# A hybrid attention and PEER layer in float32: the expert stage's schedule by fixed rules, and GpSimd's low parts on VectorE

## The reference

```python
qh = (xt @ w_query).reshape(T, PEER_HEADS, PEER_KEY_DIM)
s1 = jnp.einsum('thd,nd->thn', qh[..., :half], sub_keys_1)
s2 = jnp.einsum('thd,nd->thn', qh[..., half:], sub_keys_2)
v1, i1 = lax.top_k(s1, PEER_TOPK)
v2, i2 = lax.top_k(s2, PEER_TOPK)
cand = (v1[..., :, None] + v2[..., None, :]).reshape(T, PEER_HEADS, PEER_TOPK * PEER_TOPK)
top_s, top_j = lax.top_k(cand, PEER_TOPK)
experts = jnp.take_along_axis(cand_idx, top_j, axis=-1)
gate = jax.nn.softmax(top_s)
a = jax.nn.gelu(jnp.einsum('cd,ced->ce', xc, expert_u[experts]))
y = jnp.einsum('ce,ced->cd', gate * a, expert_v[experts])
```

## Time and profile before

| | |
|---|---|
| median of three executions | 1001.05 us |
| the three | 1001.03, 1001.05, 1006.59 us |
| the profiled execution | 1006.59 us, span 1004.7 us |
| busy share of the span | PE 98%, weight loads 86%, DVE 74%, ACT 51%, POOL 31% |
| chain that ended last | 88% of the span is L473, the matmul helper |

### The profile page before, as it was taken

How to read it: one execution, slowest core, us unless ns; L and a number is a source line. 1 busy time by engine, 2 the same in 40 slices (tenths; PEclk the granted TensorE clock), 3 DMA queues, 4 the chain that set the end, 5 groups by cost and what they waited for, 6 DMA issues and landing times.

```text
span 1004.7 us, 17520 instructions
## 1 busy us (share of the span) xinstructions
PE 986.5 (98%) x6258; PEld 865.1 (86%) x6258; DVE 745.7 (74%) x1865; ACT 517.3 (51%) x1107; POOL 311.6 (31%) x370
## 2 busy tenths in 40 slices
PE   8999999999999999999999999999999999999996
PEld 3467865999999999999999999988888888888885
DVE  1167353789999788889999999766666766666668
ACT  1245342233445788888888888543334333343341
POOL 1000000000220699999999999000000000000000
PEclk9999899999999999999999999999999999999998
DMA  9833200683555455445454454665555555556551
GB/s 328 330 125 148 84 22 1 213 320 124 183 190 179 157 169 168 164 153 168 167 166 155 166 168 157 242 231 193 197 196 189 193 198 195 191 189 195 201 169 43
DMA packets 48758, 176.52 MB, mean 176 GB/s; under 512 B 5136, under 2 KB 6176, under 8 KB 47520
## 3 DMA queue, kind: packets, MB, share of 16 engines
q1 hardware_dynamic: 48272, 173.82, 50.6%
q0 software_dynamic: 400, 1.58, 0.4%
HBM read 174.33 MB, written 1.05 MB: 175 GB/s over the span
## 4 chain that ended last, share of the span: by engine, by line
PE 90%; DVE 7%; ACT 1%; issue 1%; DMA 1%; SPq 0%; DVEq 0%
PE ps L473 88%; DVE lo L1491 1%; PE ps L657 1%; DVE pair L1679 1%; DVE arena L1624 1%; DMA arena<-in_w_tok 1%; DVE hi L1491 1%; DVE arena L1629 0%; DVE arena L1632 0%; ACT hi L1050 0%; DVE slab L1689 0%; DVE xs L1768 0%; DVE xs L1762 0%; DVE arena L1756 0%; DVE xs L1753 0%
## 5 line engine op out<-in xcount | busy, mean ns | idle before, releaser
L473 PE MATMUL ps<-x1hl,hi 128*128 128x256 f32 x2248 | 374.1, 283 | 0.6 <-DVE hi L1491 0.6
L473 PEld LDWEIGHTS ps<-x1hl,hi 128*128 128x128 f32 x2248 | 330.4, 192 | 0.9 <-DVE hi L1491 0.8
L473 PE MATMUL ps<-hi,ahl 128*128 128x512 f32 x992 | 265.3, 389 | 0.0
L1198 ACT CAST hi<-slab 128x1024 fp32r<-128x1024 f32 x128 | 135.0, 1055 | 204.8 <-PE ps L473 204.6
L473 PE MATMUL ps<-x1hl,lo 128*128 128x256 f32 x824 | 233.2, 283 | 0.0
L473 PEld LDWEIGHTS ps<-hi,ahl 128*128 128x128 f32 x992 | 186.1, 188 | 38.7
L455 POOL TENSOR_SCALAR hot<-slab 128x128 fp32r<-128x128 f32 x224 | 197.7, 898 | 0.0
L473 PEld LDWEIGHTS ps<-x1hl,lo 128*128 128x128 f32 x824 | 158.2, 192 | 0.0
L1712 DVE TENSOR_TENSOR lo<-slab,hi 128x1024 fp32r<-128x1024 f32 x128 | 156.0, 1218 | 0.0
L473 PE MATMUL ps<-lo,ahl 128*128 128x512 f32 x496 | 152.8, 389 | 0.0
L1491 DVE TENSOR_TENSOR lo<-slab,hi 128x1024 fp32r<-128x1024 f32 x97 | 121.8, 1257 | 18.9 <-ACT hi L1050 18.4
(11 more groups left out here) (199 smaller groups left out, 910.2 us busy)
## 6 DMA issues: line engine op xcount, KB each, us to landing
slab<-in_uT SPq DMA_DIRECT2D x128, 512.0 KB, 3.3
slab<-in_pv SPq DMA_DIRECT2D x128, 512.0 KB, 3.3
arena<-in_wq SPq DMA_DIRECT2D x32, 512.0 KB, 4.8
arena<-in_w_tok SPq DMA_DIRECT2D x2, 2048.0 KB, 16.3
arena<-in_w_out SPq DMA_DIRECT2D x1, 4096.0 KB, 13.7
arena<-in_w_tok SPq DMA_DIRECT2D x4, 512.0 KB, 8.4
arena<-in_w_tok SPq DMA_DIRECT2D x1, 1792.0 KB, 19.1
slab<-in_xT SPq DMA_DIRECT2D x4, 256.0 KB, 7.4
```

The costliest lines, as they stand in the source:

```text
L473: return nc.tensor.matmul(o, lhsT, rhs, start=start, stop=stop, skip_group_check=True)
L1198: nc.scalar.copy(hi[:, v_hi_slot(c), :], raw[:, v_slot(c), :]).then_inc(v_hi, 1)
```

## The change

Three things change together. The table FILL_AT and the step counter go: each place in the routing code now has a fixed rule for whether a low part is made there (`fills`, or a condition on the half t). GpSimd makes no low parts any more; VectorE makes all. And the numbers of the schedule differ: N0 33 to 41, NROUTE 29 to 36, NTURN 30 to 37, and the groups stand at 41 + g*21//16, which like before ends at block 123. In the first half (t = 0) five low parts are made, in the eight sub-key calls of the second half two each, in its route() fifteen.

```diff
-N0 = 33
-NROUTE = 29
-NTURN = 30
-FILL_AT = (54, 55, 57, 66, 68, 68, 76, 79, 79, 86, 89, 89, 97, 99, 99, 106, 109, 109, 119, 120, 120, 123, 124,
...
+N0 = 41
+NROUTE = 36
+NTURN = 37
...
-POOL_LOW = range(5, 26, 3)
-GROUP_AT = [N0 + g * (123 - N0) // 63 for g in range(GN)]
+GROUP_AT = [N0 + g * 21 // 16 for g in range(GN)]
...
-            for c in POOL_LOW:
-                pool.wait_ge(u_hi, c + 1)
-                nc.gpsimd.tensor_tensor(u_rest_of(c), u_raw(c), hi[:, c % UH, :].bitcast(F32), ALU.subtract
-                                        ).then_inc(u_lo_pool, 1)
             pool.wait_ge(table_ready, 1)
...
             def expert_in(c):
-                if c in POOL_LOW:
-                    pe.wait_ge(u_lo_pool, pool_lows(c))
-                else:
-                    pe.wait_ge(u_lo, c + 1 - pool_lows(c))
+                pe.wait_ge(u_lo, c + 1)
...
-                    if c not in POOL_LOW:
-                        dve.wait_ge(u_hi, c + 1)
-                        v.tensor_tensor(u_rest_of(c), u_raw(c), hi[:, c % UH, :].bitcast(F32), ALU.subtract).then_inc(u_lo, 1)
+                    dve.wait_ge(u_hi, c + 1)
+                    v.tensor_tensor(u_rest_of(c), u_raw(c), hi[:, c % UH, :].bitcast(F32), ALU.subtract).then_inc(u_lo, 1)
                     filled[0] += 1
 
-            steps = [0]
-
-            def pace():
-                steps[0] += 1
-                while filled[0] < NROUTE and FILL_AT[filled[0]] == steps[0]:
-                    fill()
-
-            def top16(jobs):
+            def top16(jobs, fills):
                 for o in (0, 8):
                     for vals, _, s in jobs:
                         did(v.max(vals[:, o:o + 8], s))
-                    pace()
+                    if o and fills > 2:
+                        fill()
                     settle()
                     for vals, idx, s in jobs:
                         did(v.max_index(idx[:, o:o + 8], vals[:, o:o + 8], s))
-                    pace()
+                    if fills:
+                        fill()
                     if o == 0:
                         settle()
                         for vals, _, s in jobs:
                             did(v.match_replace(s, vals[:, 0:8], s, TAKEN))
-                        pace()
+                        if fills > 2:
+                            fill()
...
-                top16([(tv[:, hh, :], ti[:, hh, :], cand[:, hh, :]) for hh in range(PH)])
+                if t:
+                    fill()
+                settle()
+                top16([(tv[:, hh, :], ti[:, hh, :], cand[:, hh, :]) for hh in range(PH)], 4 * t)
...
-                    pace()
+                    if t or part and h0:
+                        fill()
...
                     did(v.tensor_reduce(tfp, eqh, AX_X, ALU.add))
-                    pace()
+                    fill()
...
-                subkey_tops(1, b)
+                subkey_tops(1, b, 2)
```

More of the change, by code:

```diff
@@ L37 @@
 PI_IN = 3.1415925
-N0 = 33
-NROUTE = 29
-NTURN = 30
-FILL_AT = (54, 55, 57, 66, 68, 68, 76, 79, 79, 86, 89, 89, 97, 99, 99, 106, 109, 109, 119, 120, 120, 123, 124,
-           124, 127, 128, 129, 130, 131,)
+N0 = 41
+NROUTE = 36
+NTURN = 37
 GN = S // 4
@@ L321, in peer_layer_kernel @@
         u_hi, u_lo, v_hi, v_lo = sem("u_hi"), sem("u_lo"), sem("v_hi"), sem("v_lo")
-        u_lo_pool = sem("u_lo_pool")
         pe_h, gelu_done, pre_gated, gated = sem("pe_h"), sem("gelu_done"), sem("pre_gated"), sem("gated")
@@ L355, in u_rest_of @@
             return lo[:, b, :] if b < 4 else hi[:, 3, :]
-        def pool_lows(c):
-            return sum(b <= c for b in POOL_LOW)
         def v_slot(c):
@@ L1513, in top16, with subkey_tops @@
                             did(v.match_replace(s, vals[:, 0:8], s, TAKEN))
-                        pace()
+                        if fills > 2:
+                            fill()
                     settle()
-            def subkey_tops(t, b):
+            def subkey_tops(t, b, fills):
                 dve.wait_ge(sk_saved, 2 * PH * t + b + 2)
-                top16([(V[:, t, i, :], IX[:, t, i, :], sc[t][:, i, :]) for i in (b, b + 1)])
+                top16([(V[:, t, i, :], IX[:, t, i, :], sc[t][:, i, :]) for i in (b, b + 1)], fills)
             dve.wait_ge(trig, 2)
@@ L1594, in _ @@
             for b in range(0, 10, 2):
-                subkey_tops(0, b)
+                subkey_tops(0, b, 0)
             def route(t):
@@ L1700, in block_gate @@
                 v.tensor_tensor(a, gel[:, c % 2, 0:n], a, ALU.mult).then_inc(gated, 1)
-            assert filled[0] == NROUTE and steps[0] >= FILL_AT[-1]
+            assert filled[0] == NROUTE
             while filled[0] < N0 - 1:
```

## The result

The changed kernel takes 1011.61 us (median of 4, 1011.3 to 1012.46) beside 1002.63 us (median of 4, 1001.03 to 1006.59) for the kernel before: a ratio of 1.0084, 95% interval 1.0058 to 1.0109. It is slower, by a little less than 1%. The profiled execution took 1011.38 us, its span 1009.5 us.

The account below looks back on a forecast made before the run. GpSimd, nearly level with TensorE in the gates' stage, would set the pace: start at 355.4 us plus 283.6 us of work puts the last gates at 639.2 instead of 632.22, +7.0 on 1001.05, so 1008.0 us, range 1003 to 1014.

Parts of the forecast that it names:

- VectorE keeps up in routing: Routing window: VectorE makes all 36 low parts, 84.8 us of work for 89.3 us of blocks, without TensorE waiting.
- the 0.73 us: TensorE's wait before 327.92 us for a late VectorE low part in the kernel before; forecast to go.
- The margin of 0.8 us at the second routing pass: Start of second routing pass, the tightest place: VectorE 2.2 us late, under the 3.0 us of room.
- Transposes at block 37: Route transposes move from block 30 to 37, starting at 349.96 us; routes ready some 7 us ahead.
- GpSimd's first one-hot 5.4 us after the transposes, and its end as start plus work: Gates' stage: GpSimd starts at 355.4 us, 21.1 later, and ends at 639.0 after 283.6 us of work.
- A wait at block 40 of about 1 us: ScalarE's pairs stand ahead of block 40's cast; low part ready at 360.3 us, block due at 359.3.
- GpSimd's 283.6 us, 4.43 a group: Gates' stage: 290.6 us of GpSimd work less eight subtractions at 0.87 us; always behind, it no longer waits.
- Nothing after the last gates differs: After the last gates, block 123 in both kernels, no difference; loads keep their order and move with TensorE.
- B (TensorE stays the bound): Gates' stage: GpSimd's two buffers absorb the closer gates; -1.6 us, 999.4 us, up to +4; chance 0.17.
- C (no relief): GpSimd bound, the eight fewer subtractions give nothing back; +14.0 us, 1015 us; chance 0.16.
- D (VectorE late in routing): Routing: the 0.8 us margin fails, TensorE waits 1 to 3 us, GpSimd starts later; 1009 to 1011 us; chance 0.05.
- Slower by over 1%: Whole kernel: C, and the top of A (GpSimd bound, with relief) and D in a slow stretch; chance 0.21.

Follow-up runs that it names:

- after_pool_low: The changed kernel with GpSimd making the low parts of blocks 5, 8, ... 23 again; ratio to the kernel before 1.0092.
- after_early: The changed kernel with routes transposed at block 35 instead of 37 and VectorE's tables ahead of low parts 38 and 39; ratio to the kernel before 1.0082.
- after_wide38: The changed kernel with N0 38 and NTURN 35, groups spread over blocks 38 to 123; ratio to the kernel before 1.0056.
- after_act_more: The changed kernel with ScalarE making one one-hot in every group, so GpSimd has 320 instructions instead of 352; ratio to the kernel before 1.0008.
- after_wide_act: after_wide38 with ScalarE also making one one-hot of every group (GpSimd 320 instructions); ratio to the kernel before 1.0000.

## Why the prediction was right

The change itself is +6.98 us from block 0 to the end, where the sum said +7.0. On the median the kernel takes 1011.61 us, where 1008.0 stood: 3.6 more, inside the range of 1003 to 1014. The miss is in the base. The forecast stood on a median of 1001.05, the middle of three executions of which two, by their times, had lost almost nothing in the head. The four executions of the changed kernel lie within 1.2 us of the profiled one, which lost 3.5 us there. The kernel before was run again beside the experiments, 19, 25 and 23 times on three chips, with medians of 1004.37, 1004.35 and 1004.57 us; the forecast's +7.0 on those is 1011.4 to 1011.6.

1. *VectorE keeps up in routing*: right. TensorE has no wait over 0.08 us from block 0 to the transposes, and the 0.73 us are gone. The margin of 0.8 us at the second routing pass was real and small: `after_pool_low` broke it.
2. *Transposes at block 37*: right. What follows them fell where it should.
3. *GpSimd's first one-hot 5.4 us after the transposes, and its end as start plus work*: the start was right (111.90 after block 0 for 112.0), and so was the end. But the sum held one of two conditions. GpSimd's end is also the first gates, less the lead of two groups, plus the work, and `after_early` shows it: 5.7 us of the start given back, and the end stays. The changed kernel starts GpSimd 8.0 us ahead of the first gates, just the time of two groups, so both sums give one number there; that they do is luck of the forecast, not its reasoning. Seen from the gates, they begin 23.1 us later than before (119.93 for 96.79), while the stretch from the first to the last, which GpSimd's work sets, shrinks by 16.2 only (292.0 to 275.9). The difference is the 7.0.
4. *A wait at block 40 of about 1 us*: right. 1.04 us by the count of starts, behind the ScalarE casts at 355.78 and after that waited for their turn behind the pairs:

```profile
354.39 0.69 ACT L1160 ACTIVATE pair<-pair,slab 128x128 fp32r<-128x128 f32 x2 [2.17 <-POOL pair L444]
...
355.78 1.03 ACT L1036 CAST hi<-slab 128x1024 fp32r<-128x1024 f32 x1
```

5. *GpSimd's 283.6 us, 4.43 a group*: right, 283.63, with waits of 0.2 where none were forecast, but by two errors that cancel. The forecast took eight subtractions away at 0.87 us each, 7.0 us. Eight go at the front, and one (block 123) comes in at the end, since GpSimd's end now lies a block later: VectorE makes 84 low parts (68 `lo` and 16 `hi`) beside GpSimd's one-hots where it made 91 (73 and 18), seven fewer. They gave back 290.6 - 283.4 = 7.2 us, 1.03 each. Over the whole stage, with 0.58 us for a free one-hot, it is (290.6 - 352 x 0.58)/91 = 0.95 us in the kernel before and (283.4 - 352 x 0.58)/84 = 0.94 now. VectorE's three at once beside GpSimd's second group cost a little less each:

```profile
356.08 1.17 POOL L444 TENSOR_SCALAR pair<-slab 128x128 fp32r<-128x128 f32 x2
357.24 4.87 POOL L448 TENSOR_SCALAR hot<-slab 128x128 fp32r<-128x128 f32 x4
...
356.84 3.70 DVE L1476 TENSOR_TENSOR lo<-slab,hi 128x1024 fp32r<-128x1024 f32 x3 [2.63 <-ACT hi L1036]
```

Four instructions in 4.87 us where four free ones take 2.34: 2.5 more for three subtractions, 0.84 each. In TensorE's terms 7.5 us of waits stand ahead of gates in 12 places and 1.04 at block 40, 8.5 against the 9.6 of the forecast; the rest lies in pauses of under 0.2 us around gates, which a count of waits over 0.19 misses.
6. *Nothing after the last gates differs*: right. 1004.7 - 632.22 = 372.5 us in the kernel before, 1009.5 - 637.00 = 372.5 now.

Of the rivals, B (TensorE stays the bound) fell with GpSimd's waits of 0.2 us; C (no relief) with 283.6 us of work, where it began to decide at 286.6, though `after_wide38` shows 4.50 us a group, in its range, and of the gating products that it named L1678's cost GpSimd nothing that shows and L1685's little (the 12 one-hots beside one of these and no low part or L1678 take 0.67 us on average, 0.80 at most, for 0.58); D (VectorE late in routing) did not come, and did in `after_pool_low`, at the place and with the kind of price it named. Slower by over 1% did not come either, by little: the interval reaches to 1.0109.

What stays open: the 1.6 us more of GpSimd's work in `after_wide38` than its low parts explain, and the 7 us by which its work fell further than counted in `after_act_more`.

## What to carry to other kernels

When work is packed closer for one engine, compute the pace that the engine feeding it can keep, from its time per item in the stage and not from its busy share of the whole: 31% of the program was 98.6% of the stage. An engine behind double buffers has no end of its own: take the later of (its start + its work) and (first use, less the lead that the buffers allow, + its work), and try both before naming a cause. And where runs scatter by more than the change is worth, find the point in the trace where the scatter lies, and count from behind it.

## What the runs showed of the hardware

- A VectorE `tensor_scalar` of 128x1024 float32 (one SBUF input) takes 0.68 to 0.74 us and costs GpSimd 0.54 to 0.59; one of 128x128 costs it nothing that shows. The subtraction of 128x1024 with two SBUF inputs takes 1.22 us when nothing is beside it and costs GpSimd 0.84 to 1.03, 0.95 on average; a gating product with two SBUF inputs (L1678), up to 0.73 us long, costs it nothing that shows.
- It works in the other direction on a small instruction too: a VectorE cast of 256 columns, 0.29 us alone, took 2.51 beside a GpSimd subtraction of 2.40. So a short instruction that starts just behind a long one of the other engine can pay nearly the whole length of it.
- TensorE's granted clock dropped in some executions between 90 and 110 us and in others not, in the same code ahead of any edit: over 97.4 to 104.1 us it is 0.50, the lower level of 1.2 GHz, in the kernel before and the changed one, and 1.00 over 97 to 104 in `after_wide_act`. TensorE was busy for 8.24, 8.24 and 8.27 of the 10 us from 80 on and all through 90 to 96.6 in the three, so its work before the drop doesn't tell them apart. The 5.0, 3.5 and 0 us that the three profiles lose by it are about the 5 us by which the executions of this kernel scatter.
